# A two-stage transformer kernel on one core: attention scores in two reduced-precision passes, and the layer boundaries of block 2 put in another order

## The reference, cut to what matters

```python
for i in range(DEPTH_2):                       # 4 layers, kinds A B C A
    sh, sc, gt = split(silu(c) @ ada_w[i] + ada_b[i], 3)     # the "ada" rows
    h = rms_norm(x, norm_g[i]) * (1 + sc) + sh               # context tokens alike
    u, z = split(h @ w_in, [n_mix_cols])                     # u: q, k, v;  z: gate
    o, oc = (mixer_a, mixer_b, mixer_c)[kind](u, uc, ...)
    x = x + gt * ((o * silu(z)) @ w_out)
# each mixer: q, k = rms_norm per head (A and C: then rope);
#   p = softmax(q k^T / 8 [+ bias in B]);  o = p v
#   C: two maps a head, o = (p0 - lam * p1) v, then a norm of o
```

## Time and profile before

| | |
|---|---|
| median of three runs | 2466.03 us (2460.39 to 2472.28) |
| the profiled execution | 2468.51 us, span 2466.4 us |
| busy share of the span | PE 90%, PEld 75%, DVE 53%, ACT 42%, POOL 37% |
| mean granted TensorE clock | 0.932 of full |
| scores of block 2, latent tiles (L727) | 256 instructions, 153.9 us |
| scores of block 2, context tiles (L729, L730) | 192 instructions, 64.2 us |
| block 2 | from 986 us to the end, 60% of the span |

### The profile page before, as it was taken

One profiled execution on the slowest core, in us unless ns is written; L12 is line 12 of the kernel. 1 busy time (PEld: TensorE's weight loads), 2 busy tenths in 40 slices (PEclk: granted clock), 3 DMA queues, 4 the chain that ended last, 5 costly groups with the idle time before them and its releaser, 6 DMA issues.

```text
span 2466.4 us, 39608 instructions
## 1 busy us (share of the span) xinstructions
PE 2223.9 (90%) x14736; PEld 1854.9 (75%) x14736; DVE 1314.5 (53%) x2688; ACT 1033.0 (42%) x1978; POOL 912.5 (37%) x588
## 2 busy tenths in 40 slices
PE   6969899998788998899999898999889899888898
PEld 5868899987788998667766876776778566666677
DVE  4594556547844664356651235556224766723565
ACT  4433466453435654533322244332334445425332
POOL 0444378005453840333422133332313434333443
PEclk8989999989899999899979999999989899888898
DMA  6423556653345655311122321112232111223121
GB/s 220 146 85 107 187 174 193 188 171 113 103 128 172 196 189 188 120 35 44 41 88 68 120 86 56 61 52 73 86 106 92 52 43 35 79 76 120 52 69 52
DMA packets 72848, 262.92 MB, mean 107 GB/s; under 512 B 8032, under 2 KB 10208, under 8 KB 72416
## 3 DMA queue, kind: packets, MB, share of 16 engines
q1 hardware_dynamic: 71392, 256.31, 32.5%
q0 software_dynamic: 1280, 4.20, 0.6%
HBM read 259.43 MB, written 1.05 MB: 106 GB/s over the span
## 4 chain that ended last, share of the span: by engine, by line
PE 65%; DVE 18%; issue 6%; ACT 6%; POOL 5%; DMA 0%; DVEq 0%; ACTq 0%; SPq 0%; POOLq 0%
PE gemm L421 13%; PE gemm L422 12%; PE gemm L423 12%; PE gemm L688 6%; PE score L727 5%; DVE r L1348 3%; PE obank L759 3%; PE tbank L657 3%; DVE d L1294 2%; PE stat L668 1%; PE obank L763 1%; POOL arena L1830 1%; POOL w_lo L294 1%; DVE zt L1256 1%; DVE small L1554 1%
## 5 line engine op out<-in xcount | busy, mean ns | idle before, releaser
L294 POOL TENSOR_TENSOR w_lo<-ring,w_hi 128x1024 fp32r<-128x1024 f32 x252 | 605.6, 2408 | 556.0 <-ACT w_hi L874 554.7
L421 PE MATMUL gemm<-g_hi,w_hi 128*128 128x256 f32 x1344 | 395.2, 294 | 42.3 <-POOL w_lo L294 28.1
L421 PE MATMUL gemm<-h_hi,w_hi 128*128 128x512 f32 (+1 forms) x928 | 388.5, 419 | 12.4 <-DVE h_lo L1635 9.6
L874 ACT ACTIVATE w_hi<-ring 128x1024 fp32r<-128x1024 f32 x344 | 361.7, 1053 | 81.3 <-PE gemm L423 39.9
L422 PE MATMUL gemm<-g_lo,w_hi 128*128 128x256 f32 x1344 | 383.9, 286 | 0.0
L423 PE MATMUL gemm<-g_hi,w_lo 128*128 128x256 f32 x1344 | 383.8, 286 | 0.0
L422 PE MATMUL gemm<-h_lo,w_hi 128*128 128x512 f32 (+1 forms) x928 | 353.1, 381 | 0.0
L423 PE MATMUL gemm<-h_hi,w_lo 128*128 128x512 f32 (+1 forms) x928 | 352.8, 380 | 0.0
L421 PEld LDWEIGHTS gemm<-g_hi,w_hi 128*128 128x128 f32 x1344 | 264.7, 197 | 62.2 <-POOL w_lo L294 36.2
L1189 ACT ACTIVATE pr<-score,small 128x512 f32<-128x512 f32 (+1 forms) x192 | 128.0, 669 | 392.8 <-DVE small L1556 390.5
L421 PEld LDWEIGHTS gemm<-h_hi,w_hi 128*128 128x128 f32 x928 | 180.5, 195 | 148.4 <-issue 108.2
(11 more groups left out here) (278 smaller groups left out, 3885.4 us busy)
## 6 DMA issues: line engine op xcount, KB each, us to landing
ring<-wall SPq DMA_DIRECT2D x478, 512.0 KB, 3.7
r<-nbias POOLq DMA_DIRECT2D x16, 256.0 KB, 3.0
cst<-consts SPq DMA_DIRECT2D x1, 2340.5 KB, 10.3
r<-x_t SPq DMA_DIRECT2D x1, 1024.0 KB, 4.7
x<-ctx_t SPq DMA_DIRECT2D x1, 1024.0 KB, 15.5
y_t<-x SPq DMA_DIRECT2D x4, 256.0 KB, 2.3
d<-pos SPq DMA_DIRECT2D x1, 128.0 KB, 10.2
```

Source lines behind the costliest of these rows:

```text
L294: eng.tensor_tensor(w_lo[:, q % SPLITS, :, :], ring[:, t % RING, :, :], w_hi[:, q % SPLITS, :, :].bitcast(F), ALU.subtract)\
L421: pe.matmul(out, w[0][:, k, :], x[0], start=start, stop=False)
L874: act.activation(w_hi[:, q % SPLITS, :, :], ring[:, t % RING, :, :], ACT.Copy).then_inc(S["hi_ready"], 1)
```

## The change

1. Scores. `qT` gives way to `q_both`: for each of the two heads of a chunk, 64 partitions hold the high part of q and the other 64 its low part. The high part of k is stored twice (`k_twice`), the low part once (`k_low`, in place of k). A score is now q_both (128 rows) against k_twice, plus q high (64 rows) against k_low: two `fp32r` passes in place of one `f32` matmul. ACT makes the high parts (4 instructions a key chunk, 2 a query chunk), DVE the low parts of q (2), POOL those of k (2).
2. Query chain. The next query chunk is read out one unit earlier (`q_evac_at`), its rope starts one unit earlier, and the low parts are formed at the end of the last unit. In B and C key chunk c+1 is split within step c.
3. Filler. The gate chunk of step c is computed in step c instead of c-1, so the last step has a gate chunk; of the two `ada` rows one moves to step 0.
4. Boundary. ACT squares `x2[m-1]` and PE sums it after output chunk m; the table load moves ahead of the output chunks; one DVE operation of the root runs beside ACT; PE waits for `h_full` chunk by chunk and for `h_ctx` only from token tile 2.
5. The high parts of `gated` move from DVE to ACT.

```diff
@@ PE, block2
-        pe.wait_ge(S["roped"], rbase(L) + nk + c + 1)
+        pe.wait_ge(S["q_split"], L * KC + c + 1)
+        pe.wait_ge(S["k_split"], kbase(L) + (nk if kind == "A" else c + 1))
-    q = qT[a:a + HD, c % 2, :]
-    if t < 2:
-        ins = pe.matmul(bk[:, :], q[:, t * P:(t + 1) * P], kT[a:a + HD, kc, :], start=True, stop=True)
...
+    q = q_both[:, c % 2, us[u][1], :]
+    kh, kl = k_high(kind, kc, us[u][1]), k_low[a:a + HD, kc, :]
+    for tile_, to, at, w in ((t, 0, 0, N2),) if t < 2 else ((2, 0, T, C), (3, C, T, C)):
+        pe.matmul(bk[:, to:to + w], q[:, tile_ * P:(tile_ + 1) * P], kh[:, at:at + w], start=True, stop=False)
+        ins = pe.matmul(bk[:, to:to + w], q[a:a + HD, tile_ * P:(tile_ + 1) * P], kl[:, at:at + w], start=False, stop=True)
...
         if c + 1 < KC:
+            yield from chunk(h(NQ), NQ, None, early if c == 1 else None)
+        if c == 1 and slot:
+            ada_columns()
+        if c:
             yield from chunk(h(NQ), NQ)
-            yield from chunk(h(NQ), NQ)
-        else:
-            for _ in range(FILL_SLOT[L]):
-                yield from ada_row()
+        if c in (0, KC - 1) and slot:
+            early = n["tile"]
+            yield from row_tiles(1 if c == 0 else 2)
...
     for m in range(2, KC):
         run(chunk(h(NQ), NQ))
+        if need_ctx:
+            if m == 2:
+                square_sum(L + 1, 0)
+            square_sum(L + 1, m - 1)
@@ ACT, block2
+    def q_split_high(c):
+        R = rbase(L) + nk + c
+        if kind != "B":
+            act.wait_ge(S["roped"], R + 1)
+        for hh in range(2):
+            a = HD * hh
+            ins = act.activation(q_both[a:a + HD, c % 2, hh, 0:NQ], raw[a:a + HD, R % 2, 0:NQ], ACT.Copy)
+        ins.then_inc(S["q_hi_ready"], 1)
...
-            if u == NU // 2 and c + 1 < KC:
-                evac_q(c + 1)
+            if u == 1 and kind != "A" and c + 1 < KC:
+                k_split_high(c + 1)
+            if u == min(q_evac_at(NU) + 2, NU - 1) and kind != "B" and c + 1 < KC:
+                q_split_high(c + 1)
+            if u == q_evac_at(NU) and c + 1 < KC:
+                evac_q(c + 1, early if c == 1 else None)
@@ DVE, block2
+    def q_split_low(c):
+        dve.wait_ge(S["q_hi_ready"], L * KC + c + 1)
+        for hh in range(2):
+            a, to = HD * hh, HD * (1 - hh)
+            ins = dve.tensor_tensor(q_both[to:to + HD, c % 2, hh, 0:NQ], raw[a:a + HD, R % 2, 0:NQ],
+                                    q_both[a:a + HD, c % 2, hh, 0:NQ].bitcast(F), ALU.subtract)
...
         if u == NU - 1 and c + 1 < KC:
-            q_rms(c + 1)
+            q_split_low(c + 1)
```

More of the change, by code:

```diff
@@ L131, in tile_plan @@
         put("k", L, "P" * nk)
-        put("qz", L, "PP" * KC)
-        put("last", L, "RRRR" * FILL_SLOT[L])
-        put("w_out", L, "P" * KC)
+        row = "RRRR" if FILL_SLOT[L] else ""
+        put("qz", L, "PPPP" + row + "P" * 12)
+        put("w_out", L, "PP" + row + "P" * 6)
     assert len(plan) == N_TILES
@@ L788, in gemm_part @@
                         nonlocal spot
-                        for _ in range(spot * count // parts, (spot + 1) * count // parts):
+                        if 0 < c < KC - 1:
+                            steps = (spot + 1) * count // parts - spot * count // parts
+                        elif spot < parts // 2:
+                            steps = KC // (parts // 2) + (spot < KC % (parts // 2))
+                        else:
+                            steps = (spot + 1) * 8 // parts - spot * 8 // parts
+                        for _ in range(steps):
                             next(pieces, None)
@@ L847, in seq, with op @@
                 act.wait_ge(S["act_step"], n["step"])
-            def op(tiles=1, at=None):
+            def op(tiles=1, at=None, ahead=AHEAD):
                 n["tile"] += tiles
@@ L1137, in evac_z, with gated_high @@
                     act.sem_inc(S["z_evac"], 1)
+                def gated_high(c):
+                    act.wait_ge(S["gated_ready"], L * KC + c + 1)
+                    act.activation(h_hi[:, c, 0:NQ], gated[:, place(c, nk), 0:NQ], ACT.Copy).then_inc(S["gated_hi"], 1)
                 turned_n = tbase(L)
@@ L1168, in block2 @@
                 act.wait_ge(S["roped"], rbase(L) + nk)
+                for j in range(2 if kind == "A" else 1):
+                    k_split_high(j)
+                if kind != "B":
+                    q_split_high(0)
                 evac_z(0)
+                early = None
                 for c in range(KC):
                     for u in range(NU):
-                        if u == 0 and c:
-                            evac_z(c)
+                        if u == 0 and c >= 2:
+                            evac_z(c - 1)
                         U = ebase(L) + c * NU + u
@@ L1641, in block2 @@
                 past = [None] * 4
-                n_split = 0
                 for c in range(KC):
```

243 lines of the change are left out of this document (172 added, 71 removed).

## The result

The changed kernel takes 2627.06 us, median of four runs (2623.33 to 2627.25), against 2463.21 us for the kernel before (2459.72 to 2472.28): a ratio of 1.0656, 95% interval 1.0623 to 1.0688. The profiled execution has a span of 2624.9 us, 158.5 more than the 2466.4 of before. The forecast was 2438.

The account below looks back on a forecast made before the run. PE work was taken to bound the middle steps, chains and thin PE work the last steps. Terms: -102 + 73 + 4 + 10 + 7.5 - 21 = -28.5 us, giving 2438 for the median; range 2403 to 2472.

Parts of the forecast that it names:

- term 1: Scores, all layers: two reduced passes replace one full-precision product, saving 0.58 us in each of 176 units, -102 us.
- term 2: Changes of step: PE waits for q's low-part subtractions, 1.9 us in layers 0 and 1; +73 us, plus 4 for the clock.
- (c): Rival, layers 0, 1 and 3: the clock falls after every new wait, 21 steps, 32 us more, 2470; chance 12%.
- (d): Rival, changes of step: low-part subtractions fall under a POOL instruction, 2 us in 21 steps, +42, 2480; chance 10%.
- 512 columns on 64 partitions cost as much as on 128: Subtractions of q's low parts: row length sets the cost, 0.61 us each; bounds half of that and twice.
- about 3: Sign, layer 3: a wait of about 3 us before the first score of a step.
- 28 to 30: Sign, layer 2: steps of 28 to 30 us, against 26.3 and 27.8 in the kernel before.
- Term 3: First score of a layer: ACT's key copies and POOL's subtractions come before it, +10 us.
- Term 4: Layer boundaries: gain 12.4, loss 16.2 from sums waiting for squares, 3.8 lost three times; +7.5 us with the entry.
- The gain of 3.9 at the entry: Into layer 0: the table load, the DVE operation and the earlier start give 3.9 us.
- Term 5: Filler: gate chunk moved from step 0 to the last step, an `ada` row to step 0; -21 us.

Follow-up runs that it names:

- e7: Changed kernel with the first pass of a score on 64 rows too, q's low-part product left out, run for its rows alone: 2608.91 us, one execution.
- e2: Changed kernel with the low pass of each score over all 128 rows instead of 64: 2557.11 us, ratio 1.0388 to the kernel before.
- e4: Changed kernel with low pass over 128 rows and q's two low-part subtractions ahead of the last read-out: 2500.83 us, ratio 1.0157 to the kernel before.
- e3: Changed kernel with DVE's two low-part subtractions of the next q ahead of a step's last read-out of the values: 2536.81 us, ratio 1.0304.
- e1: Changed kernel with scores back to one full-precision product, no splits of q and k, the rest as changed: 2506.56 us, ratio 1.0160.
- e5: e4 plus boundary sums two chunks behind, layer 2's q read out a unit later, layer 3's third output tile's high part early: 2475.69 us, ratio 1.0042.
- the fastest version: Last gate product on POOL held until DVE's first low parts, against the kernel with layer 2's sine product ahead of the key split: 2414.00 us, ratio 0.9795.
- e6: e5 with DVE's shuffle and cosine product of the next q ahead of the copy of the transposed block: 2456.93 us, ratio 0.9968.

## Why the prediction was wrong, step by step

The sum was -28.5 us, the profiled executions are 158.5 apart. Of the 187 between them 101 lie in the middle steps of layers 0 and 1, forecast at 26.3 and 26.0 us, which is 24 less in all, and measured 77 longer. Two steps of the prediction failed there: the price of a 64-row pass (term 1) and the length of the wait for the subtractions (term 2).

**Term 1, the scores: -102, measured -19. Failed.** By the rows after, 128 units of 512 columns save 1.05 - 0.84 = 0.21 (27 us) and 48 context units lose 0.17 (8 us). The step that failed is "A reduced pass with 64 rows is not in the trace; I take it at the price of 128 rows", with its lower bound of 48: the pass costs little, the change of rows around it 0.2 (e7). The kernel before had a sign of it, though not in the 0.34 of the earlier trace rows, which I put down to the change of mode: there a pass behind full-precision transposes of 128 rows has 0.31 as well (1119.36 to 1119.67). The sign is in its weight loader, at the exit of a 64-row score:

```profile
1117.50 0.19 PEld L421 LDWEIGHTS gemm<-h_hi,w_hi 128*128 128x128 f32 x1 [0.76 <-issue]
```

The load starts with the pass and not ahead of it. e2 gives 70 us back where 83 are missing, but some 17 of them are the wait in layer 1; e4's rows show the forecast price of 128-row passes to be right.

**Term 2, the wait: +73 and +4 for the clock. Failed in size, and rivals (c) and (d) happened together.** Forecast 1.9 us in layers 0 and 1, found 3.95; "POOL has done its root by then and waits for the next ACT split" was true, and that split comes at just that moment, since ACT makes it right behind the last exponential of the step. I should have looked up when POOL's next `w_lo` starts, not only that it was idle. The clock fell in most of these steps. Together 5.1 and 5.7 us a step (e3: 76 us in layers 0 and 1), where the forecast had 1.7 and 1.9. Nor does the bound of rival (d) come out of its own sum: 1.4 us in 21 steps is 2467, and a slower kernel (2478) needs 1.9. "512 columns on 64 partitions cost as much as on 128" held (1.41 for two). In layer 3 the wait of "about 3" held (3.0 to 4.1). Layer 2 has steps of 29.7 us (from 2042.53 to 2250.40 in seven), inside "28 to 30", but 22 us more in all, where none was forecast (33, less the 28 of its scores and 5 of filler).

On DVE and POOL the trace first: 1.41 us for the pair with POOL behind it, 3.43 with POOL beside it, 0.54 behind POOL's end. The Trainium skill, "SBUF — State Buffer", Who interferes with whom, says that a VectorE instruction with two SBUF inputs contends with a GpSimd instruction that reads SBUF, and that the shared ports are an exclusive lock; the trace agrees, three times (q's low parts, the rope's addition, `h_lo` in the last step).

**Term 3, first score: +10, measured +12.7, but right by accident.** e1 shows 352.3 without splits against 363.3 before, and 376.0 with them: the splits cost 24, and the rearranged start of the layer gives 11, which stands in no term of the forecast. In layer 0 these are 8.39 us instead of 10.18 for the first 64 value products and a wait of 3.10 instead of 5.23 ahead of the first score; why the wait fell was not tested.

**Term 4, the boundaries: +7.5 (+11.4 without the entry), measured +12.9 without the entry. Right.** PE, ACT and DVE at the end of layer 0, after:

```profile
1365.88 1.13 PE L696 MATMUL stat<-sq,cst 128*128 128x512 f32 x2 [1.75 <-ACT sq L1135]
1374.36 1.12 PE L696 MATMUL stat<-sq,cst 128*128 128x512 f32 x2 [1.75 <-ACT sq L1135]
1399.17 0.69 DVE L1816 TENSOR_TENSOR x<-x,rot 128x512 f32<-128x512 f32 x1 [7.84 <-ACTq L1343]
1412.53 7.68 PE L729 MATMUL gemm<-ring,arena 128*128 128x128 f32 x51 [0.25 <-DMA ring<-wall]
```

Chunks 8.48 us apart (8.6 forecast), waits of 1.75 and 1.81 (1.97), and the first value product behind the condition rows' transfers, 13.4 us after the last addition. Forecast 3.8 lost per boundary, found 4.3. The gain of 3.9 at the entry cannot be told from block 1's spread. e5 takes the waits away: 32 us.

**Term 5, the filler: -21, measured a loss of about 14 and more. Failed.** Forecast 30 us for the last step of layer 0; it took 38.1. The gate chunk in its first half reads `h_hi` and `h_lo`, so the seven splits of `gated`, which before began in the first unit, all fall into the last three, beside POOL (4.44 us above), and PE waits 4.39 for the exponentials behind them. In layer 1 the condition row, moved into step 0, waits for its transfer, and in layer 3 the third output tile has no low part:

```profile
1321.93 1.12 PE L689 MATMUL tbank<-cst,pr 128*128 128x128 f32 x4 [4.39 <-ACT pr L1293]
1584.64 1.03 PE L497 MATMUL gemm<-ring,sc_c 128*2 128x128 f32 x16 [6.64 <-DMA ring<-wall]
2601.71 0.58 PE L453 MATMUL gemm<-h_hi,w_hi 128*128 128x256 f32 x1 [4.74 <-POOL w_lo L305]
```

I counted PE's work that leaves a step and not the ring's slots and the low parts on which the moved work depends. That step 0 is long because of the row is read from the traces alone (34.5 and 37.9 us in layers 0 and 1, before 28.0 and 29.8; in e1, with the scores as before, 30.5 and 33.1, of which PE waits 2.0 and 2.3 for a `w_lo` and 1.8 and 1.2 for transfers); no run undid it.

Layer 2 is the part that I understand least: the rearrangement alone costs 17 us there (e1), a later read-out of q is no cure, and 13 us stay open in the fastest version. Ten of these lie in the last five of its seven middle steps, 28.7 to 29.4 us each. There PE waits 12.7 us in all for ACT's read-out and square of q and 10.5 for ACT's exponentials, where the kernel before waited 1.0 and none, and 8.7 for the rope. So ACT, which has the new high parts to make, is the likely cause; this is read from the trace and not tested.

## What to carry to other kernels

Price a new matmul by the start of the instruction behind it in a row of the same shape, and treat each change in the number of rows, full to half or back, as a cost of its own: padding the short pass to full rows was worth 70 us here, about 17 of them because the passes' shorter time also moved a collision. Two repairs that can touch the same wait are priced together and not added. Before placing vector work with two inputs at the end of a step, look up which instruction the general engine starts at that moment and what releases it; moving two subtractions ahead of one read-out gave 90 us. Where work moves into a step, write down which buffers it keeps, since what needs those buffers is squeezed into what is left of the step.

## What the runs showed of the hardware that I had not expected

- Weight loads go under a running pass of the same number of rows (128 rows: starts 0.23 us apart for 512 columns, 0.12 for 256; 64 rows: 0.12 for 256), but not under one with another number of rows (0.41 to 0.43, and 0.31; idle loader of 0.24 to 0.37). The Trainium skill, "TensorE: Matmul & The Clock Gate", The mechanism, says in one sentence that a load overlaps running matmuls only when its row group differs, and in another that a load into the background weight buffer is pulled ahead too. Here same rows overlap, which only the second allows, and the 64 rows inside the 128 do not; where the first sentence differs, the measurement decides.
- After a wait of 3.95 us 512-column passes 0.43 us apart (half the clock) stand in the first 6.5 us of most steps, and the granted clock of the step is 0.90 to 0.93; waits of 0.3 to 1.05 us in layer 0 left it at 1.00 (e6, e3, e4), those of 1.29 in layer 1 too (e4), those of 1.92 gave 0.94 (e2).
- A subtraction of 64 partitions into the other 64 costs 0.70 us for 512 columns (e3), no more than an addition of 128x512 that stays in place (0.69).
